# Moving the two-expert unit of a mixture-of-experts stage from second to sixth place, and unrolling the units on TensorE

## The reference, cut to what matters

```python
def expert_block(args):
    tok, e = args
    xb = xt[tok]
    gt, up = jnp.split(xb @ w_gate_up[e], 2, axis=-1)
    return (jax.nn.silu(gt) * up) @ w_down[e]
y = yb.reshape(cap, d) * slot_w[:, None].astype(h.dtype)
out = jax.ops.segment_sum(y, slot_tok, num_segments=n)
```

## Time and profile before

| | |
|---|---|
| median of three runs | 1320.05 us |
| the profiled execution: its time | 1322.77 us |
| the profiled execution: its span | 1321.0 us |
| TensorE matmul busy | 1122.3 us, 85% of the span |
| TensorE weight loads busy | 508.0 us, 38% |
| VectorE busy | 419.2 us, 32% |
| ScalarE busy | 199.8 us, 15% |
| GpSimd busy | 165.7 us, 13% |
| mean granted TensorE clock | 0.933 of full speed |
| read from HBM | 460.73 MB, 350 GB/s over the span |

### The profile page before, as it was taken

How to read it: one execution, slowest core, us unless ns; L and a number is a source line. 1 busy time by engine, 2 the same in 40 slices (tenths; PEclk the granted TensorE clock), 3 DMA queues, 4 the chain that set the end, 5 groups by cost and what they waited for, 6 DMA issues and landing times.

```text
span 1321.0 us, 18125 instructions
## 1 busy us (share of the span) xinstructions
PE 1122.3 (85%) x7434; PEld 508.0 (38%) x7435; DVE 419.2 (32%) x855; ACT 199.8 (15%) x439; POOL 165.7 (13%) x186
## 2 busy tenths in 40 slices
PE   9999999997966696669899999999978765875597
PEld 6445546433321232123264455463333212331232
DVE  5899733311110110011185996232111101110111
ACT  4423404000000000000054224030000000000000
POOL 1767300000000000000044762000000000000000
PEclk9999999999887897789999999999989877987899
DMA  8433687999999999999964316969999999999997
GB/s 289 169 128 128 255 345 292 364 435 424 432 431 424 433 433 429 425 430 423 403 212 174 129 78 255 399 258 419 428 422 434 430 429 428 432 434 427 426 420 290
DMA packets 60833, 462.72 MB, mean 350 GB/s; under 512 B 20360, under 2 KB 20576, under 8 KB 40288
## 3 DMA queue, kind: packets, MB, share of 16 engines
q1 hardware_dynamic: 59728, 461.70, 84.6%
q10 hardware_dynamic: 1040, 0.09, 0.1%
HBM read 460.73 MB, written 1.05 MB: 350 GB/s over the span
## 4 chain that ended last, share of the span: by engine, by line
PE 62%; DMA 32%; SPq 3%; issue 1%; DVE 0%; ACT 0%; DVEq 0%
DMA pool_all<-in_w_gate_up_dram 30%; PE ps L1125 23%; PE ps L850 9%; PE ps L884 4%; PE ps L724 4%; PE ps L909 3%; PE ps L1139 3%; PE ps L703 2%; PE ps L734 2%; PE ps L865 2%; DMA pool_all<-in_w_down_dram 2%; SPq L627 1%; PE ps L1043 1%; SPq L538 1%; PE ps L1075 1%; PE ps L768 1%
## 5 line engine op out<-in xcount | busy, mean ns | idle before, releaser
L1125 PE MATMUL ps<-pool_all,xs 128*32 128x512 f32 (+1 forms) x2816 | 334.0, 634 | 168.2 <-DMA pool_all<-in_w_gate_up_dram 168.0
L1125 PEld LDWEIGHTS ps<-pool_all,xs 128*32 128x32 f32 x2816 | 91.1, 116 | 405.2 <-issue 404.6
L1929 DVE SCALAR_TENSOR_TENSOR rope<-rope,ps 128x512 f32<-128x512 f32 x22 | 15.1, 688 | 525.3 <-ACT rope L1473 525.3
L1139 PE MATMUL ps<-pool_all,early 128*32 128x512 f32 (+1 forms) x1408 | 156.9, 594 | 20.7 <-ACT early L1475 13.6
L850 PE MATMUL ps<-pool_all,hT 128*128 128x512 f32 x256 | 114.6, 598 | 0.0
L1473 ACT ACTIVATE rope<-ps 128x512 f32<-128x512 f32 x22 | 13.1, 597 | 637.6 <-PE ps L1125 637.6
L1139 PEld LDWEIGHTS ps<-pool_all,early 128*32 128x32 f32 x1408 | 44.3, 110 | 118.8 <-issue 117.4
L2200 POOL TENSOR_TENSOR pool_all<-pool_all 128x512 f32<-128x512 f32 x64 | 79.9, 1281 | 36.5 <-DVE pool_all L1705 36.5
L1075 PE MATMUL ps<-xs,cst 128*128 128x512 f32 x176 | 81.4, 605 | 0.0
L1043 PEld LDWEIGHTS ps<-cst,hT 128*128 128x128 f32 x640 | 73.0, 192 | 16.8 <-issue 16.8
L1043 PE MATMUL ps<-cst,hT 128*128 128x128 f32 x640 | 76.8, 278 | 0.0
(11 more groups left out here) (261 smaller groups left out, 1020.1 us busy)
## 6 DMA issues: line engine op xcount, KB each, us to landing
pool_all<-in_w_gate_up_dram SPq DMA_DIRECT2D x46, 4096.0 KB, 26.2
pool_all<-in_w_down_dram SPq DMA_DIRECT2D x58, 2048.0 KB, 22.4
pool_all<-in_w_gate_up_dram SPq DMA_DIRECT2D x18, 2048.0 KB, 11.8
pool_all<-in_w_in_dram SPq DMA_DIRECT2D x12, 2048.0 KB, 11.6
pool_all<-in_w_gate_up_dram SPq DMA_DIRECT2D x24, 1024.0 KB, 14.6
pool_all<-in_w_gate_up_dram SPq DMA_DIRECT2D x24, 512.0 KB, 12.8
pool_all<-in_w_glu_dram SPq DMA_DIRECT2D x4, 2048.0 KB, 10.5
pool_all<-in_w_out_dram SPq DMA_DIRECT2D x4, 2048.0 KB, 12.6
```

The source lines that it names most:

```text
L1125: mm = pe.matmul(ps[r, half], xT[:, k // 4, k % 4, r], lane_cols(n, h, k % 4, half), start=(k == 0), stop=(k == KC - 1), skip_group_check= ...
L1139: mm = pe.matmul(ps[r, 2 + half], ffT[:, c, r], lane_cols(n, 2, c, half), start=(c == 0), stop=(c == 3), skip_group_check=True)
```

## The change

It has five parts.

1. **Order of units.** The duo becomes unit 5 (`MIDDLE`); `trio_of(u)` gives the trio of a unit. SyncE's order is written anew: behind unit 0 come parts of unit 1 and of unit 2; behind each half of unit 1's gate and up products come three single parts (two of unit 2, and a home part of unit 3). Unit 5 has no home pair (`HOMES`). `load_rest(5)` loads the duo's two pairs, its two down parts, and the first down part of unit 6; `load_rest(6)` loads only two down parts. `load_home(6)` follows `load_rest(4)`, `load_home(7)` follows `load_rest(5)`, and `load_home(8)` follows `load_rest(7)`. The bytes stay the same: 96 parts a layer.
2. **Spare lane of unit 0.** Expert 0 always gets it (`rank`), so unit 0 reads no register, and its pick matrix is made from `slot_of` at once, in two comparisons of 128 columns.
3. **Gather of unit 0.** k = 0 and k = 1 are gathered one by one, each with its own signal and copy; k = 2 and 3 between the products of k = 0 and k = 1; k = 4 to 7 between the two halves. One of the four copies of `keep_x` moves there too.
4. **TensorE's units** are no longer a loop but straight code, and the waits for weights come from a table of constants (`LANDED`). SyncE's loop is unrolled as well; VectorE keeps a loop for units 1 to 3.
5. **ScalarE** issues the six small transfers of the next layer's gains and vectors (`load_gain`, `load_rows`) earlier, in the middle of layer 0's second norm and not behind the routing.

```diff
+MIDDLE = 5
+HOMES = (0, 9, 0, 9, 0, None, 9, 0, 9, 0, 9)
...
-    put("rank", TRIO - 1 - np.arange(EXPERTS) % TRIO)
+    put("rank", TRIO - 1 - np.arange(EXPERTS) % TRIO + 8 * SEQ * (np.arange(EXPERTS) == 0))
...
+    def trio_of(u):
+
+        return u if u < MIDDLE else u - 1
...
+    LANDED = (((0, 1), (3, 1), (6, 1)), ((4, 1), (7, 1)), ((2, 1), (5, 1), (8, 1))), \
+        (((9, 1), (3, 4), (6, 4)), ((10, 1), (4, 3), (7, 3)), ((2, 2), (5, 2), (8, 2))), \
...
-                for e, index in ((0, duo + 1), (1, second + 1), (2, second + 2)):
+                for e, index in ((1, first(1) + 1), (2, first(1) + 2), (0, first(2))):
                     load_piece(part_slot(part, e), index, part, a, b, landed[part_slot(part, e)])
             sp.wait_ge(unit_used, at(unit_used, l, 3))
             sp.sem_inc(settled, 1)
-            for e, index in ((0, duo), (1, duo + 1), (2, second + 2)):
-                load_part(part_slot(2, e), index, 2)
-            sp.wait_ge(unit_used, at(unit_used, l, 5))
-            sp.sem_inc(settled, 1)
-            load_pair(9, second)
-            load_pair(0, second + TRIO)
+            for e in range(TRIO):
+                load_part(part_slot(2, e), first(1) + e, 2)
+            for part in range(2):
+                sp.wait_ge(unit_used, at(unit_used, l, 4 + part))
+                sp.sem_inc(settled, 1)
+                for i, index in ((3, first(2) + 1), (6, first(2) + 2), (9, first(3))):
+                    load_part(i + part, index, part)
             sp.wait_ge(unit_used, at(unit_used, l, 6))
             sp.sem_inc(settled, 1)
-            for e in range(2):
-                load_part(part_slot(2, e), second + e, 2)
+            for e in range(TRIO):
+                load_part(part_slot(2, e), first(2) + e, 2)
...
             def load_rest(u):
-                first = l * EXPERTS + (u - 1) * TRIO
-                sp.wait_ge(unit_used, at(unit_used, l, u * 3 + (-1)))
+                sp.wait_ge(unit_used, at(unit_used, l, u * 3 - 1))
                 sp.sem_inc(settled, 1)
-                for e in (1, 2):
-                    load_pair(part_slot(0, e), first + e)
+                pairs = ((1, duo + 1), (2, duo)) if u == MIDDLE else ((1, first(u) + 1), (2, first(u) + 2))
+                for e, index in pairs:
+                    load_pair(part_slot(0, e), index)
                 sp.wait_ge(unit_used, at(unit_used, l, u * 3))
                 sp.sem_inc(settled, 1)
-                for e in range(TRIO):
-                    load_part(part_slot(2, e), first + e, 2)
-
-            with sp.Fori(0, 2) as j:
-                load_rest(j * 2 + 3)
-                load_home(j * 2 + 4, 9)
-                load_rest(j * 2 + 4)
-                load_home(j * 2 + 5, 0)
-            load_rest(BRANCH - 1)
-            load_home(BRANCH, 9)
+                if u != MIDDLE + 1:
+                    pairs += ((0, first(u + (u == MIDDLE))),)
+                for e, index in pairs:
+                    load_part(part_slot(2, e), index, 2)
+
+            load_rest(3)
+            load_home(4)
+            load_rest(4)
+            load_home(6)
+            load_rest(5)
+            load_home(7)
+            load_rest(6)
+            load_rest(7)
+            load_home(8)
...
-            keep_x(1)
+            keep_x(1, range(1))
...
+                    if first and h:
+                        keep_x(1, range(1, 2))
+                        gather_first(range(4, KC), 3, main["gathered"])
...
+                        if first and k == 0:
+                            gather_first(range(2, 4), 2, main["gathered"])
...
-            gather_first(range(0, 2), 2, first_rows)
-            gather_first(range(2, 4), 3, main["gathered"])
-            pe.wait_ge(spared, at(spared, l, 1))
-            pe.sem_inc(settled, 1)
-            unit(0, TRIO, trio_lanes(0), first=True)
-            unit(1, 2, duo_lanes)
+            for k in range(2):
+                gather_first(range(k, k + 1), 2 + k, first_rows)
+            unit(0, first_lanes)
             pe.wait_ge(spared, at(spared, l, 2))
             pe.sem_inc(settled, 1)
-            with pe.Fori(1, BRANCH // 2) as j:
-                unit(j * 2, TRIO, trio_lanes(j * 2 - 1, away=True), turn=j, away=True)
-                unit(j * 2 + 1, TRIO, trio_lanes(j * 2), turn=j)
+            for u in range(1, BRANCH):
+                unit(u, duo_lanes if u == MIDDLE else trio_lanes(u))
...
+                if t == 0 and l < DEPTH - 1:
+                    load_gain(l + 1)
+                    load_rows(l + 1)
                 x_out(t, 0, 4)
...
+            ve.tensor_tensor(slot_of, ps[:, 1, 0:64].rearrange("p (t n) -> p t n", t=NT), assign, ALU.mult).then_inc(dve_layer, 1)
             ve.scalar_tensor_tensor(trio_tmp[:, 0:EXPERTS], ps[:, 1, 64:96], 4.0, const("rank"), ALU.mult, ALU.add).then_inc(dve_layer, 1)
-            ve.tensor_tensor(slot_of, ps[:, 1, 0:64].rearrange("p (t n) -> p t n", t=NT), assign, ALU.mult).then_inc(dve_layer, 1)
+            L.add()
+            ve.wait_ge(dve_layer, L.value())
+            first_pick(0, 2, first_slots[:, :, 0:1])
+            first_pick(2, 4, first_slots[:, :, 1:3]).then_inc(main["match"], 1)
```

More of the change, by code:

```diff
@@ L393, in trunk @@
     x_rows_ready = signal("x_rows_ready", 2)
-    first_rows, first_xT = signal("first_rows"), signal("first_xT")
+    first_rows, first_xT = signal("first_rows", 2), signal("first_xT", 2)
     dve_layer, dve_list = signal("dve_layer", 187), signal("dve_list", 25)
@@ L534, in _, with first @@
                 sp.sem_inc(settled, 1)
-                load_part(9 + part, l * EXPERTS + DUO, part)
+                load_part(9 + part, l * EXPERTS + TRIO, part)
             def load_piece(i, index, part, a, b, sem):
                 sp.dma_start(wide_slot(i)[:, a:b], expert_part(index, part)[:, a:b]).then_inc(sem, 16)
-            duo, second = l * EXPERTS + DUO, l * EXPERTS + TRIO
+            def first(u):
+                return l * EXPERTS + TRIO * trio_of(u)
+            duo = l * EXPERTS + DUO
             for n, (part, a, b) in enumerate(((0, 0, 1), (0, 1, 2), (0, 2, 4), (1, 0, 2), (1, 2, 4))):
@@ L602, in _ @@
             sp.nop()
[L603 to L606, removed]
+            load_rest(8)
+            load_home(9)
+            load_rest(9)
+            last = first(UNITS - 1)
             def last_slot(part, e):
@@ L958, in positions, with keep_x @@
                     pe.matmul(ps[:, 1, 64:96], const("ones"), assign[:, 1], start=False, stop=True, skip_group_check=True).then_inc(pos_mm, 1)
-            def keep_x(t):
-                for half in range(2):
+            def keep_x(t, halves=range(2)):
+                for half in halves:
                     pe.matmul(ps[:, 4 + 2 * t + half], const("ident"), xs[:, t, 512 * half:512 * half + 512],
@@ L1078, in scatter, with unit @@
                             mm.then_inc(x_sum, 1)
-            def unit(i, experts, lane_cols, first=False, last=False, turn=0, away=False):
-                def landed_by(slot, loads, run=0):
-                    pe.wait_ge(landed[slot], at(landed[slot], l, run * 16 + 16 * (front_loads[slot] + loads)))
+            def unit(i, lane_cols):
+                first, last = i == 0, i == UNITS - 1
                 def arrived(part):
[L1086 to L1102, removed]
+                    for slot, loads in LANDED[i][part]:
+                        pe.wait_ge(landed[slot], at(landed[slot], l, 16 * (front_loads[slot] + loads)))
                 def tail(n):
@@ L1107, in unit @@
                 for h in range(2):
-                    if first and h == 0:
-                        pe.wait_ge(first_xT, at(first_xT, l, 1))
-                    else:
+                    if first and h:
+                        keep_x(1, range(1, 2))
+                        gather_first(range(4, KC), 3, main["gathered"])
+                    if h or not first:
                         pe.wait_ge(main["xT"], at(main["xT"], l, 2 * i + (h + 1)))
@@ L1116, in unit @@
                     for k in range(4 * h, 4 * h + 4):
+                        if first and k < 2:
+                            pe.wait_ge(first_xT, at(first_xT, l, k + 1))
                         if first and k == 2:
-                            gather_first(range(4, KC), 2, main["gathered"])
                             pe.wait_ge(main["xT"], at(main["xT"], l, 1))
@@ L1185, in pair, with trio_lanes @@
                 scatter(S, i)
-            def trio_lanes(i, away=False):
-                spare = pe.value_load(spare_at[0:1, bass.ds(i, 1)], min_val=0, max_val=TRIO * SLOT * (TRIO - 1))
-                spare_0 = pe.value_load(spare9_at[0:1, bass.ds(i, 1)], min_val=0, max_val=SLOT * 9) if away else spare
+            def trio_lanes(u):
+                i, away = trio_of(u), HOMES[u] == 9
+                spare = pe.value_load(spare_at[0:1, i:i + 1], min_val=0, max_val=TRIO * SLOT * (TRIO - 1))
```

(25 more changed lines are left out.)

59 lines of the change are left out of this document (24 added, 35 removed), and 9 rows, old and new, of the table LANDED.

## The result

The changed kernel takes 1342.01 us at the median of six runs (1341.56 to 1342.75); the kernel before took 1321.17 us on the same chip (1319.96 to 1322.18). The ratio is 1.0159, 95% interval 1.0149 to 1.0169: 20.8 us slower. The profiled execution took 1342.02 us with a span of 1340.1 us. The profiled execution of before, 1322.77 us, lies above the highest of its six timed runs, so a difference of the two spans (19.1 us) shows a little too little.

What follows compares the result with a forecast made beforehand. The expert stage was taken to be bound by DMA transfers of expert weights. Start -3.8, gap +16.5 and fetch +5.3 sum to +18.0 us, from 1320.05 to 1338.0 us; own range 1332 to 1343.

Steps and rivals of the forecast that it cites:

- part 1: Way into unit 0: its k = 0 products end 1.9 us earlier per layer, so transfers start earlier; -3.8 us in all.
- the three releases: Before unit 0's gather: TensorE free at 228.90, comparisons out by 228.8, ScalarE's x_rows ending 228.78; gather starts at 228.99 us.
- Part 2: Small unit in sixth place: DMA queue runs empty behind unit 6's pairs, 8.25 us per layer, +16.5 us in all.
- my bound of 16.15: Longest gate and up half in the rows, in us, used for the upper bound of 8.5 us on the gap.
- Part 3: TensorE's middle units as straight code: 16 more instruction packets at 0.33 us each, +5.3 us; bounds 0 and 17.6.
- (a): Rival for the whole kernel: the gap opens and the instruction fetch is hidden, 1332.8 us; chance 0.12.
- (b): Rival for the middle units: the instruction fetch costs full price, +17.6 us, giving 1350 us; chance 0.04.
- (c): Rival at unit 6: no gap opens; 1316.3 us, or 1321.6 with the fetch's 5.3; chance 0.07.
- (d): Rival at unit 0: the start gains nothing, through the wait for the pick or a queue hole; 1341.8 us, chance 0.07.

Runs made afterwards that it cites:

- order_only: The changed kernel with part 1 undone (old way into unit 0; new order and written-out loop kept): 1345.04 us, ratio 1.0187 to the kernel before.
- start_straight: The kernel before with part 1 and TensorE's loop written out, the two-expert unit staying second: 1323.74 us, ratio 1.0028 to the kernel before.

## Why the prediction was right, and where its terms were off

The forecast was 1338.0 us, 18.0 slower than the 1320.05 it started from; measured were 20.8. The three parts can now be priced from the kernels, each against before in its own session: the written-out loop +4.1 (mean of 3.4, 4.4 and 4.4), the new order 24.0 - 4.1 = +19.9, part 1 in the new order 20.8 - 24.0 = -3.2. The last two carry about 2 us either way, by the intervals of the ratios. The price of the new order holds all that order_only has beside the written-out loop: the table of waits, SyncE's loop written out and ScalarE's earlier issues were not run by themselves.

**Part 1, the start: forecast -3.8, measured -3.2 in the new order.** The end of k = 0 came 1.68 us earlier against the start of keep_x, not 1.9: the two single gathers took 1.12 us together where I had put 1.01, and the products of k = 0 took 1.92 where I had put 1.79. The rest held: the three releases met, the later end of unit 0 opened no hole, ScalarE's issues (202.97 to 205.39 us) lay in the idle time. What I did not see is that this gain belongs to the new order only. I said of the old order that its queue is never empty, which is true of before, and overlooked that it has next to nothing to spare: two signals, the ends of unit 1's and unit 2's gate and up products, come just as the queue runs low. An earlier start makes the queue run dry there, while those two signals themselves come about 1 us later, since unit 0 ends later; in the old order part 1 gave a loss of 1.6 us. The three kernels with no, one and two signals relieved show it step by step, 1.0012, 0.9998 and 0.9983, and the first relief alone does nothing (1.0004). The dip behind the first pieces of layer 0, which stands only where part 1 meets the old order, takes a further part, and its cause is open. So the new order did repair something, although I had denied it ("nothing is gained for it"); it is small beside what it costs.

**Part 2, the hole: forecast +16.5, measured +19.9.** Place, cause and neighbours were right: against the start of keep_x, unit 3's half begins 12.6 us later (345.42 - 228.88, before 331.96 - 228.00; forecast 12.7); the only two holes stand behind unit 6's pairs, at 484 to 497 us (forecast 487 to 495) and at the like place of layer 1, and they shrink when the slots are freed earlier. The size is the term that was mis-sized. It is best taken from one landing to the next. Forecast were 16.0 us up to the freed slots, less 9.75 us of queued work, plus 1.95 us of restart: 8.25 per layer. In layer 0 TensorE's half took 0.24 + 16.82 us, as more than 5 us of it ran at the lower of its two clocks (granted 0.50 up to 484 us in the windows above), and the landing came at 517.28, 21.87 us behind TensorE's end at 495.41, which is 2.4 more than the 19.5 of its own bytes. In layer 1 it was 0.24 + 15.56 us and 22.23, so 2.7 more. That makes 9.7 and 8.8 us. So the restart, with the signals at both its ends, was 0.4 to 0.8 us longer than assumed, and the half of layer 0 1.0 us longer; my bound of 16.15 for it was too low, since the loop of before has a half of 16.85 us, shown above at 331.96.

One thing I got wrong without its changing the sum. The pairs of unit 6 landed at 451.51 + 26.84 = 478.35, and I let the two down parts flow for 9.75 us from there, to 488.1. The rate fell already between 484 and 486 us. From the landing to 488.00 the rate was 307 GB/s, 6.9 us' worth of the 9.75, so nearly 3 us of that work had flowed before the semaphore of the older transfer came. It is not a late semaphore. In the packet records of the trace each transfer ends with sixteen packets of 4 bytes, by my reading one for each DMA engine. For unit 6's last pair they lie between 474.32 and 477.90 us, and the landing comes 0.45 us behind the last, within the "up to 1 us" of the forecast. The engines were 3.6 us apart, and a landing waits for the last of them. The last of the two down parts' closing packets is at 487.70, close to the 488.1 of the forecast. Behind the hole the engines are in step again: for unit 7's last pair the packets lie between 516.38 and 516.92. That is why the bytes between the two landings (301 and 314 GB/s on average in layers 0 and 1, against 430) leave 11.7 and 10.2 us unused, while the landings lose only 9.7 and 8.8. The two cadences together are 18.5 of the 19.9; the remaining 1.4 is within the 2 us of uncertainty, and the runs do not show what it is. The 17.1 us between start_straight and the changed kernel are the same 19.9 less the 3.2 that part 1 gains in the new order alone.

**Part 3, the fetch: forecast +5.3, measured +4.1.** The count of packets was right, 64, and the longer cadences stand in the middle units, as forecast. The price per packet is 0.26 us (4.1 by 16), against the 0.33 I took from ten packets. (My remark that the loop's rounds moved no packets does not fit my own count: three of the ten fell in them.) That the packets themselves are the cause is argued from where they stand, not shown: the runs meant to add packets and nothing else failed to do so. What the runs show is that the written-out loop costs 4 us. That the forecast lies near it speaks for the count of packets only if the packets are the cause; otherwise it is partly luck. The sum, too, was helped by errors that partly cancel: 0.6 us too much gain from the start and 3.4 us too little loss from the hole, against 1.2 us too much loss from the fetch. The Trainium skill (Runtime: NRT & Kernel Launch, Instruction fetch mechanics) calls the cost of block crossings mostly hidden and prefers full unrolling; here three runs put unrolling at 1.0025, 1.0032 and 1.0035, where TensorE had some 12 us of waiting per unit to hide it in. So unrolling was not free in this stage, whatever the cause.

**The rivals.** (a), fetch hidden, and (b), full price, are both out by the runs of the written-out loop, which cost 4.1 us and not 0 or 17.6. (c), no hole, fell with the profile. (d), the start gains nothing, was wrong for this kernel; in the old order the start gains nothing, but mainly through signals that the rival did not name.

## What to carry to other kernels

In a stage bound by transfers, count for each landing how many bytes are still queued and how long the slots behind them stay taken; here a smaller unit in the middle let the loader run ahead, and then the buffer, and no longer the bandwidth, set the pace of the next unit. An earlier start is only worth something if every later signal has slack for it: look for the signals at which the queue is nearly dry. Where the queue is short, issue weights in the grain in which slots come free (halves, not pairs). And measure before writing out a loop on an engine that waits anyway: here it cost 4 us and gained nothing.

## What the runs showed of the hardware

With a full queue the closing packets of one transfer lay 3.6 us apart, and nearly 3 us of the work behind it had flowed when its semaphore came; behind a time with an empty queue they lay 0.5 us apart. With an empty queue, four parts landed 21.9 and 22.2 us behind the end of the products that freed their slots, 2.4 and 2.7 us more than their 19.5 us at 430 GB/s. Written-out code cost time on an engine that was not the bound, 4.1 us, with 16 more packets of instructions. A row of 256 semaphore increments took TensorE 38 us, about 0.15 us each, too long to be used as padding. And the cadence of units with equal bytes is not smooth: it is mostly 43.8 to 43.9 us, or 0.2 to 1.7 us more, and what lengthens it is not shown.
